# A fixed spacing of the weight blocks in SBUF: 528 bytes instead of 512

## What is computed

```python
h = rmsnorm(x, norm_mix[l]); proj = h @ w_in[l]
...
x = x + merged @ w_o[l]
x = x + conv_ffn(h, ffn_w_in[l], ffn_conv_w[l], ffn_conv_b[l], ffn_w_out[l])
...
x = x + FFN_HALF * swiglu(rms_norm(x, norm_g[layer, 0]), ffn_w13[layer, 0], ffn_w2[layer, 0])
```

## Time and profile before

| what | value |
|---|---|
| median of three runs | 3283.96 us |
| lowest, highest | 3273.26, 3284.52 us |
| span of the profiled execution, first to last instruction | 3281.5 us |
| mean granted TensorE clock of that execution | 0.980 of 2.4 GHz |
| TensorE matmul busy | 3186.0 us (97%), 13833 matmuls |
| VectorE / ScalarE / GpSimd busy | 1850.9 / 923.5 / 346.3 us |

### The profile page before, as it was taken

How to read it: one execution, slowest core, us unless ns; L and a number is a source line. 1 busy time by engine, 2 the same in 40 slices (tenths; PEclk the granted TensorE clock), 3 DMA queues, 4 the chain that set the end, 5 groups by cost and what they waited for, 6 DMA issues and landing times.

```text
span 3281.5 us, 37188 instructions
## 1 busy us (share of the span) xinstructions
PE 3186.0 (97%) x13833; PEld 2526.1 (77%) x13833; DVE 1850.9 (56%) x2389; ACT 923.5 (28%) x1243; POOL 346.3 (11%) x160
## 2 busy tenths in 40 slices
PE   8989999999999999999998999999999999999999
PEld 6767567877788887888877788887888887588887
DVE  8796435437776655554476755445454446465432
ACT  2443233323222222222222322222222234322222
POOL 2334014022000000000023000002000031000000
PEclk9999889999999999999999999999999998999999
DMA  3222002321323222223332222232223321022232
GB/s 129 78 77 90 26 32 90 116 77 61 119 91 99 96 97 91 90 96 99 102 107 77 77 96 96 97 103 95 96 96 99 105 76 46 7 97 90 96 105 88
DMA packets 79372, 287.67 MB, mean 88 GB/s; under 512 B 9056, under 2 KB 9312, under 8 KB 78880
## 3 DMA queue, kind: packets, MB, share of 16 engines
q1 hardware_dynamic: 77328, 278.03, 25.7%
q0 software_dynamic: 1936, 8.13, 0.7%
HBM read 284.02 MB, written 2.10 MB: 87 GB/s over the span
## 4 chain that ended last, share of the span: by engine, by line
PE 76%; issue 14%; POOL 5%; DVE 4%; ACT 1%; DMA 0%; POOLq 0%; DVEq 0%; ACTq 0%
PE ps L589 23%; PE ps L591 23%; PE ps L590 23%; POOL w_lo L543 5%; PE ps L682 1%; PE ps L1066 1%; PE ps L698 1%; PE ps L927 1%; PE ps L748 0%; PE ps L1065 0%; PE ps L1072 0%; DVE rstd L1566 0%; ACT w_hi L1110 0%; DVE w_lo L1502 0%; PE ps L933 0%
## 5 line engine op out<-in xcount | busy, mean ns | idle before, releaser
L589 PE MATMUL ps<-h_hi,w_hi 128*128 128x512 f32 (+1 forms) x2443 | 966.9, 396 | 33.8 <-POOL w_lo L543 20.8
L590 PE MATMUL ps<-h_lo,w_hi 128*128 128x512 f32 (+1 forms) x2443 | 956.4, 391 | 0.0
L591 PE MATMUL ps<-h_hi,w_lo 128*128 128x512 f32 (+1 forms) x2443 | 955.4, 391 | 0.0
L1110 ACT ACTIVATE w_hi<-raw 128x1024 fp32r<-128x1024 f32 x525 | 555.4, 1058 | 1315.6 <-PE ps L591 1297.8
L1502 DVE TENSOR_TENSOR w_lo<-raw,w_hi 128x1024 fp32r<-128x1024 f32 x390 | 476.9, 1223 | 450.3 <-ACT w_hi L1110 449.8
L589 PEld LDWEIGHTS ps<-h_hi,w_hi 128*128 128x128 f32 x2443 | 464.2, 190 | 142.8 <-POOL w_lo L543 24.6
L591 PEld LDWEIGHTS ps<-h_hi,w_lo 128*128 128x128 f32 x2443 | 464.0, 190 | 97.0
L590 PEld LDWEIGHTS ps<-h_lo,w_hi 128*128 128x128 f32 x2443 | 464.0, 190 | 96.5 <-issue 2.4
L589 PE MATMUL ps<-mid_hi,w_hi 128*128 128x512 f32 x1208 | 477.7, 395 | 2.0 <-DVE mid_lo L1577 2.0
L591 PE MATMUL ps<-mid_hi,w_lo 128*128 128x512 f32 x1208 | 476.9, 395 | 0.0
L590 PE MATMUL ps<-mid_lo,w_hi 128*128 128x512 f32 x1208 | 476.8, 395 | 0.0
(11 more groups left out here) (363 smaller groups left out, 2687.4 us busy)
## 6 DMA issues: line engine op xcount, KB each, us to landing
raw<-in_wstream SPq DMA_DIRECT2D x525, 512.0 KB, 3.3
x<-in_x SPq DMA_DIRECT2D x8, 256.0 KB, 5.6
x_in<-in_x POOLq DMA_DIRECT2D x8, 256.0 KB, 3.0
mem_x<-in_mem POOLq DMA_DIRECT2D x2, 1024.0 KB, 5.2
out<-x POOLq DMA_DIRECT2D x8, 256.0 KB, 3.5
tmp<-in_ret_decay POOLq DMA_DIRECT2D x1, 1024.0 KB, 5.2
rope_r<-in_rope_r POOLq DMA_DIRECT2D x1, 512.0 KB, 3.7
mats<-in_mats SPq DMA_DIRECT2D x1, 320.0 KB, 6.6
```

The lines of the kernel that those rows point to most:

```text
L589: nc.tensor.matmul(dst, hi_w, hi_x, start=first, stop=False)
L590: nc.tensor.matmul(dst, hi_w, lo_x, start=False, stop=False)
L591: return nc.tensor.matmul(dst, lo_w, hi_x, start=False, stop=last)
L1110: nc.scalar.activation(w_hi[:, n % HL], raw[:, r], ACT.Copy).then_inc(hi_ready, 1)
```

## The change

The two weight tensors get blocks of 132 columns (528 bytes), of which the first 128 are used. The slot and the block become one index. The three instructions that write or read a whole panel (ScalarE's copy, VectorE's and GpSimd's subtraction) now see it as 8 rows of 128 columns: with a step of 132 in `w_hi` and `w_lo`, of 128 in `raw`. The number of instructions, their order, semaphores and element counts stay.

```diff
-        w_hi = sb(ctx, "w_hi", [P, HL, KB * P], F32R)
-        w_lo = sb(ctx, "w_lo", [P, HL, KB * P], F32R)
+        w_hi = sb(ctx, "w_hi", [P, HL * KB, P + 4], F32R)[:, :, 0:P]
+        w_lo = sb(ctx, "w_lo", [P, HL * KB, P + 4], F32R)[:, :, 0:P]
...
+        def blocks_of_panel(buf, n):
+
+            return buf[:, n % HL * KB:n % HL * KB + KB]
+
+        def raw_blocks(n):
+            return raw[:, n % RAW].rearrange("p (k n) -> p k n", n=P)
...
-                    nc.gpsimd.tensor_tensor(w_lo[:, n % HL], raw[:, n % RAW], w_hi[:, n % HL].bitcast(F32), ALU.subtract)\
+                    nc.gpsimd.tensor_tensor(blocks_of_panel(w_lo, n), raw_blocks(n), blocks_of_panel(w_hi, n).bitcast(F32),
+                                            ALU.subtract)\
                         .then_inc(lo_by_pool, 1)
...
             def blocks(n, k):
-                sl = slice(k * P, (k + 1) * P)
-                return w_hi[:, n % HL, sl], w_lo[:, n % HL, sl]
+                return w_hi[:, n % HL * KB + k], w_lo[:, n % HL * KB + k]
...
-                nc.scalar.activation(w_hi[:, n % HL], raw[:, r], ACT.Copy).then_inc(hi_ready, 1)
+                nc.scalar.activation(blocks_of_panel(w_hi, n), raw_blocks(n), ACT.Copy).then_inc(hi_ready, 1)
...
-                v.tensor_tensor(w_lo[:, n % HL], raw[:, n % RAW], w_hi[:, n % HL].bitcast(F32), ALU.subtract)\
+                v.tensor_tensor(blocks_of_panel(w_lo, n), raw_blocks(n), blocks_of_panel(w_hi, n).bitcast(F32), ALU.subtract)\
                     .then_inc(lo_ready, 1)
```

## The result

The changed kernel takes 3308.24 us (median of four runs, 3308.09 to 3310.7) against 3282.2 us before (the three runs known already and one of 3280.44): a ratio of 1.0083, 95% interval 1.0071 to 1.0096. It is slower, by 26 us. The forecast was 3308 us with the range 3248 to 3330.

The account below looks back on a forecast made before the run. The rate at which TensorE takes matmuls was held to bound the kernel. `h` +31 and `mid`/`br` -7 gave +24 us; with 0.5 for writers, 3281.5 + 24.5 = 3306, plus 2.5 to the median, 3308 us, range 3248 to 3330.

Parts of the forecast that it names:

- The offset between weights and moving tile sets the pace: 512-column matmuls: relative place of weights and moving tile seems worth 5.7 ns each, `h` 226.7 against `mid` 232.4.
- 231.0 ns for both tiles: Dense `h` and `mid`/`br` matmuls: start distance after the change, from 226.7 for `h` and 232.6 for `mid` and `br`.
- the bounds of 230.0 to 232.4: Unsettled 512-column matmuls: at 230.0 ns the matmul terms give +12 us, at 232.4 they give +40.
- the 230 to 232 named as the sign of it: Dense `h` stretch in the changed profile: starts 230 to 232 ns apart, uneven, `mid` within 1 ns of it.
- +31: `h` matmuls: 7233 x (231.0 - 226.7) ns, +31 us.
- -7: `mid` and `br` matmuls: 4392 x (231.0 - 232.6) ns, -7 us.
- a rhythm that needs six equal distances to settle gets three: `h` matmuls: the block's remainder moves 16 bytes every three matmuls, so they stay near the unsettled 230.8 ns; 231.0 taken.
- The writers in eight rows: Panel copy and subtractions by ScalarE, VectorE, GpSimd: at most 84 ns more each, 2 us at most, 0.5 us taken.
- No change: Matmul pace: only the moving tile's own address matters, or gain and loss cancel near 229 ns; 3284 us, chance 0.27.
- Settling everywhere: Matmul pace: `h` keeps 226.7 ns, `mid` and `br` come down to it, -26 us; 3258 us, chance 0.19.
- Much faster: Matmul pace: stagger parts the two streams, 215.6 ns a matmul, 155 us less; 3129 us, chance 0.09.
- GpSimd's rival: GpSimd's panel subtraction in 8 rows takes twice as long, some 110 panels wait, 60 us; 3345 us, chance 0.03.

Follow-up runs that it names:

- The two kernels that level tiles and weights: Kernel before plus 384 unused bytes behind `small`: 3249.12 us; kernel before plus 128 bytes ahead of `w_hi`, 384 behind `w_lo`: 3296.59 us.
- two kernels with offsets in turn: Kernel before, blocks 512 bytes apart, `w_lo` 16 or 128 bytes further on, `h` and `mid` remainders kept: 3310.32 us (16), 3311.37 us (128).
- the second experiment: Kernel before with weights moved to remainder 256 by 128 unused bytes ahead of `w_hi` and 384 behind `w_lo`: 3296.59 us, ratio 1.0040.
- the first experiment: Kernel before with 384 unused bytes behind `small`, so `mid`, `br` and others start at the weight blocks' remainder: 3249.12 us, ratio 0.9908.

## Why the prediction was right

**The bound.** It is the pace of TensorE: the page, the waiters and the writers above show that no wait and no other engine took the added time.

**The offset between weights and moving tile sets the pace.** The prediction gave this 5.7 ns a matmul and left open whether the moving tile's own address was behind it. The two kernels that level tiles and weights settle it: the roles change with the weights.

**231.0 ns for both tiles.** Measured 232.1, inside the bounds of 230.0 to 232.4 and 0.1 above the 230 to 232 named as the sign of it. The size was a little short. Over all dense matmuls `h` went from 227.0 to 232.1, 7233 x 5.1 = +37 us where +31 was forecast. `mid` and `br` went from 232.9 to 232.1, 4392 x 0.8 = -4 where -7 was forecast. The sum of the two, +33, is above both the forecast +24 and the 25.0 us of the spans. The rest is in the trace, if all of TensorE's time is sorted by distance between starts: dense matmuls +27.0 us (21 fewer of them), those 250 to 440 ns apart +9.6 (26 more, ten of them at 420 to 440 ns, the pace at the 1.2 GHz level), longer pauses -5.2, the small matmuls of attention and scans -5.2, matmuls of 256 columns -1.0, the border between the two kinds -0.2. The small matmuls took 341.0 us before and 335.8 after. In the experiments' kernels, where they are the same instructions, they took 329.9 to 344.1, so a difference of 5 us can't be put down to the change. The total was hit more closely than its terms: `h` cost 6 us more than forecast and `mid` and `br` gave 3 us less back, while the shorter pauses and small matmuls took 10 us off. That the time came within 1 us of the forecast is luck.

**The reason given for 231.0 doesn't hold as it stands.** The step that fell short is "a rhythm that needs six equal distances to settle gets three". It says that the change of offset is what costs, and that it prevents settling. But a constant offset of 32, 96, 160, 192 or 224 bytes, on which the pace does settle, costs 233 to 234. And with `w_lo` 16 bytes on, where the offset changes twice in every three matmuls, five of the 21 stretches of `h` ran at 226.7 throughout. What the change does is to make each tile pass through all offsets, of which few are good: the mean of the thirteen measured levels (227.0, 228.0, 233.3, 232.7, 228.9, 230.0, 233.4, 232.1, 232.9, 234.3, 233.3, 233.3 and 226.7 for -16) is 231.2 ns. That is most of the way from 227.0 to 232.1. But the changed kernel's own distances agree with these levels only in part. By block of the two slots, from all dense stretches:

```
block j     0     1     2     3     4     5     6     7     8     9    10    11    12    13    14    15
h       227.7 229.9 230.4 233.8 232.4 230.5 233.9 232.0 234.5 232.2 232.8 230.0 233.5 232.5 232.6 234.9
mid     234.9 231.8 232.9 230.0 233.6 232.4 232.8 235.4 228.2 230.0 230.7 233.6 232.5 229.9 233.8 231.7
```

`mid` repeats `h` shifted by eight blocks, which is its 128 bytes. So the time goes by the offset here too, and at offset 0 (block 0 of `h`, block 8 of `mid`) both are near 228. Block j of `h` has the offset -16j. Against the constant offsets, eight of its thirteen comparable blocks are within 1 ns, but block 1 is at 229.9 where -16 held for a panel gives 226.7, block 2 at 230.4 where 224 gives 233.3, block 12 at 233.5 where 64 gives 228.9, and block 15 at 234.9 where 16 gives 228.0. A matmul's time thus depends on the offsets before it as well, which fits the two kernels with offsets in turn, and the closeness of 231.2 to 232.1 is a sum of misses both ways. What is shown is that the step costs and that bad offsets cost by themselves; how much of the 5.1 ns belongs to the levels and how much to the changing stays open. The offsets 144, 176 and 208 weren't tried.

**The rivals.** "No change" fell with `h` at 232.1, and its mechanism, the moving tile's own address, with the second experiment. "Settling everywhere" fell with `h` at 232.1, though a gain of that size does exist: levelling the tiles by 384 unused bytes gives 3249 us where the rival said 3258. "Much faster" fell, as none of the offsets tried comes near 216 ns. GpSimd's rival fell with its median of 2407 ns for 2399. The writers in eight rows cost nothing that can be measured; 0.5 us had been set aside.

## What to carry to other kernels

Where TensorE is the bound and every float32r matmul of 512 columns reloads its weights, place weight blocks and moving rows so that their addresses leave the same remainder by 256 bytes, and check it tile by tile: here one gap of 384 bytes per partition is worth 0.9%, and a pad between blocks costs 0.8%. Don't pad against conflicts by habit. Look for it in the distance from start to start in a dense stretch, and in more than one stretch. The mean duration of a matmul can point the wrong way: before, `mid` had 395 ns and `h` 397, though `mid` took 5.9 ns more from start to start.

## What the hardware did that I had not expected

- The pace depends on a difference of addresses, modulo 256 bytes, between two streams that TensorE reads: 226.7 ns at 0 and -16, up to 234.3 at 160, with 512 columns at the full clock. The Trainium skill, "TensorE: Matmul & The Clock Gate", section "Step-by-step: what each phase is for", has two independent read ports, so that a weight load takes nothing from the running matmul, and "SBUF — State Buffer", section "Who interferes with whom", has it that TensorE never waits on anyone. By the first no place of the weights could matter, and the runs here disagree by 7.6 ns a matmul for float32r operands. The second is about one engine against another; it counts TensorE's two read ports as independent, and no run here tests it beyond that. What is behind the dependence these runs don't show.
- One sequence of addresses can have two steady paces: 232.3 and 226.7 ns in the kernel with `w_lo` 16 bytes on, 233.3 and 226.7 for `mid` at offset 112, 232.4 and 233.3 for `mid` in the kernel before. Steady doesn't mean even. At 1205 us in the kernel before, the distances of `mid` repeat every seven matmuls, from 228 to 241 ns; at 1560 us they alternate between 229 and 238; `h` at its good pace has only 226 and 227. Whether the paces cause the spread between runs is open, since the granted clock moves too. In the kernel with `w_lo` 16 bytes on the runs spread over 17 us at 0.979 to 0.981. In the kernel before 15 runs spread over 14 us, the fastest at 0.983 and the slowest at 0.978, and the first experiment's kernel, where both tiles run at 226.7, still spreads over 10.7 us, with the two longest at 0.979 and the others at 0.981 to 0.983. The changed kernel spreads over 2.6 us at 0.981 to 0.982.
- Even the best pace has 13.3 ns over the streaming time of 213.3. None of the kernels got under 226.7 for a whole tile, and what it consists of stays open.
